# Two-tile feed-forwards opened tile by tile: h stationary, 512 weight columns moving, results turned

## The reference, cut to what matters

```python
def causal_depthwise_conv(u, w, b):        # 3 taps along the tokens, per column
    ...
def conv_glu_ffn(h, w_up_act, w_up_lin, w_conv, b_conv, w_down):
    a = causal_depthwise_conv(h @ w_up_act, w_conv, b_conv)
    return (jax.nn.gelu(a) * (h @ w_up_lin)) @ w_down
...
def _swiglu(h, wg, wu, wd):
    return (jax.nn.silu(h @ wg) * (h @ wu)) @ wd
```

## Time and profile before

| what | value |
|---|---|
| median of 3 runs | 2520.38 us (2516.61 to 2524.2) |
| the profiled execution | 2516.55 us, its span 2514.7 us |
| mean granted TensorE clock | 0.988 of full speed |
| TensorE matmul busy | 2418.3 us (96%) |
| VectorE busy | 1678.3 us (67%) |
| ScalarE busy | 1079.9 us (43%) |
| weight and modulation transfers | 418.55 MB, 49.7% of 16 DMA engines |

### The profile page before, as it was taken

One profiled execution on the slowest core, in us unless ns is written; L12 is line 12 of the kernel. 1 busy time (PEld: TensorE's weight loads), 2 busy tenths in 40 slices (PEclk: granted clock), 3 DMA queues, 4 the chain that ended last, 5 costly groups with the idle time before them and its releaser, 6 DMA issues.

```text
span 2514.7 us, 34853 instructions
## 1 busy us (share of the span) xinstructions
PE 2418.3 (96%) x13166; PEld 2033.5 (81%) x13166; DVE 1678.3 (67%) x2618; ACT 1079.9 (43%) x1850; POOL 390.8 (16%) x431
## 2 busy tenths in 40 slices
PE   6899999989999999999979999999999999999998
PEld 5678988779979888887648888889888888777997
DVE  6957987858995776777865565566565566356554
ACT  4566545566554212236744322224322225344543
POOL 1101101111111101105850110100100110001101
PEclk9999999999999999999989999999999999999999
DMA  8765895647783554543212463442353444322662
GB/s 322 248 174 188 306 322 201 220 117 247 262 278 115 184 191 173 191 153 93 68 34 84 135 197 120 164 171 94 128 203 125 155 170 114 120 90 77 194 201 93
DMA packets 135880, 422.57 MB, mean 168 GB/s; under 512 B 28448, under 2 KB 32672, under 8 KB 135712
## 3 DMA queue, kind: packets, MB, share of 16 engines
q1 hardware_dynamic: 135152, 418.55, 49.7%
q10 hardware_dynamic: 560, 1.79, 0.2%
HBM read 419.17 MB, written 1.11 MB: 167 GB/s over the span
## 4 chain that ended last, share of the span: by engine, by line
PE 66%; DVE 2%; ACT 1%; POOL 1%; issue 0%; POOLq 0%; DVEq 0%; ACTq 0%
PE ps L1141 20%; PE ps L1142 20%; PE ps L1143 20%; PE ps L1336 2%; PE ps L1324 1%; POOL ap L2208 1%; PE ps L1241 1%; PE ps L1293 1%; PE ps L1304 1%; DVE ps L2033 0%; PE ps L1359 0%; PE ps L1348 0%; ACT F L1458 0%; DVE sl L1687 0%; DVE hL L1776 0%
## 5 line engine op out<-in xcount | busy, mean ns | idle before, releaser
L1399 ACT ACTIVATE sh<-raw 128x1024 fp32r<-128x1024 f32 x534 | 551.6, 1043 | 907.1 <-PE ps L1143 880.2
L1141 PE MATMUL ps<-hH,sh 128*128 128x256 f32 (+1 forms) x2560 | 839.3, 328 | 3.7 <-DVE hL L1776 2.7
L1142 PE MATMUL ps<-hL,sh 128*128 128x256 f32 (+1 forms) x2560 | 834.5, 326 | 0.0
L1143 PE MATMUL ps<-hH,sl 128*128 128x256 f32 (+1 forms) x2560 | 834.5, 326 | 0.0
L1687 DVE TENSOR_TENSOR sl<-raw,sh 128x1024 fp32r<-128x1024 f32 x534 | 639.7, 1218 | 102.2 <-ACT sh L1399 101.9
L1141 PEld LDWEIGHTS ps<-hH,sh 128*128 128x128 f32 x2560 | 481.5, 188 | 55.5 <-issue 8.0
L1142 PEld LDWEIGHTS ps<-hL,sh 128*128 128x128 f32 x2560 | 480.7, 188 | 49.2 <-issue 1.7
L1143 PEld LDWEIGHTS ps<-hH,sl 128*128 128x128 f32 x2560 | 481.3, 188 | 48.2
L1701 DVE CUSTOM_DVE_ANT_0 mjunk<-raw,cB,V 128x1024 bf16<-128x1024 f32 x384 | 499.2, 1300 | 28.4 <-DMA C<-in_cst 8.4
L2181 POOL TENSOR_TENSOR uLl<-F,uHh 128x256 fp32r<-128x256 f32 (+1 forms) x132 | 168.1, 1274 | 1175.7 <-ACT uHh L1576 1068.0
L1141 PE MATMUL ps<-sh,uHh 128*128 128x512 f32 x792 | 311.8, 394 | 2.5 <-DVE sl L1687 2.5
(11 more groups left out here) (164 smaller groups left out, 2038.4 us busy)
## 6 DMA issues: line engine op xcount, KB each, us to landing
raw<-in_w SPq DMA_DIRECT2D x752, 512.0 KB, 4.7
G<-gates SPq DMA_DIRECT2D x14, 512.0 KB, 6.7
raw<-in_w SPq DMA_DIRECT2D x16, 256.0 KB, 4.5
cB<-in_rpb SPq DMA_DIRECT2D x64, 64.0 KB, 2.6
raw<-in_w SPq DMA_DIRECT2D x4, 492.0 KB, 5.9
S<-in_rows SPq DMA_DIRECT2D x6, 256.0 KB, 3.2
X<-in_x ACTq DMA_DIRECT2D x1, 1024.0 KB, 11.9
X<-in_ctx SPq DMA_DIRECT2D x1, 1024.0 KB, 6.0
```

What stands on the lines that cost most here:

```text
L1141: self.e.matmul(out, lh, rh, start=start, stop=False)
L1142: self.e.matmul(out, lh, rl, start=False, stop=False)
L1143: return self.e.matmul(out, ll, rh, start=False, stop=stop)
L1399: self.e.activation(self.m["sh"][k % SPL][:, 0:w], self.m["raw"][r % RAW][:, 0:w], ACT.Copy).then_inc(self.sems["w_hi"], 1)
```

## The change

In a two-tile feed-forward, column blocks 0 to 3 of both matrices are made in another way (`by_tile`). Their eight units are cut as two k-blocks by 512 columns. h of one tile is held stationary and 512 weight columns move, six matmuls for each unit and tile, so the result has tokens on its partitions. Each of the four results (two matrices, two tiles) is copied from PSUM to `S` (`utok`, two copies on ScalarE, two on VectorE) and turned back by four transposes (`uturn`) into four banks, each of which holds two column blocks. Tile 0 begins before tile 1 is turned: three units of `w_up_act` for tile 0, then tile 1's turn, then the fourth unit and two of `w_up_lin` for tile 0, and so on. In front of it stand 7 warming matmuls in `ffn1` and 14 in the last feed-forward, in place of 14 and 5.

The gated units of column blocks 0 to 3 follow beside column blocks 4 and 5 in `ffn1`: blocks 0, 1 and 4 beside block 4, and 2, 3 and 5 beside block 5. In the last feed-forward all four come one behind the other. `pace` is not called for the first four blocks; for the other 18 its argument is 2 x 22/18. The list `aside` begins with 5 empty entries instead of 8.

In the mixer's output projection, uppers are held back (`hold`) from the first use of tile 1 on; `ready` lets one go behind tile 0's split and one in front of tile 1's scaling, and `lowers` sends the owed lowers. Tile 0's split now stands ahead of tile 1's `gate2` (also in the down parts of `ffn1`, which share `gate_half`).

```diff
-    def norm_tile(self, hid, t, AB, s, st=None, wide=False, lag=0, early=False):
+    def norm_tile(self, hid, t, AB, s, st=None, wide=False, lag=0, early=False, held=False):
...
             self.second_parts()
+        if held:
+            self.add("lowers")
+            self.add("ready", n=1)
...
-    def gate_half(self, t, half, b, gid, AB, hid, st2):
+    def gate_half(self, t, half, b, gid, AB, hid, st2, held=False):
...
         self.rms_close(st2[t], 2)
+        self.second_parts()
+        if held and t:
+            self.add("ready", n=1)
...
-        self.norm_tile(hid, t, AB, 0, st, early=True)
+        self.norm_tile(hid, t, AB, 0, st, early=True, held=held and t)
...
                     part(kp, half, taken[(kp, half)], [i], i == 1, banks[half][i] if kp == 3 else None)
-                self.gate_half(i, half, banks[half][i], gid, AB, hid, st2)
+                    if i and not half and kp == 2:
+                        self.add("hold", on=True)
+                self.gate_half(i, half, banks[half][i], gid, AB, hid, st2, True)
...
+    def by_tile(self, names, hid, warm):
+
+        take = lambda n, j: self.unit(True, [n + (k, 0, 512) for k in (2 * j, 2 * j + 1)])
+
+        def part(n, j, t, b, last):
+            self.add("down", unit=n, ks=[2 * j, 2 * j + 1], tiles=[(t, (t, b))], last=last, full=b if j == 3 else None,
+                     act=("h", hid), nk=KD)
+
+        def stage(t, b, on):
+            S = self.place("S", 2 + t)
+            self.add("utok", b=b, S=S, on=on)
+            self.left(b)
+            return S
+
+        def turned(t, S, to):
+            self.add("uturn", S=S, t=t, to=to)
+
+        self.warm(warm)
+        self.add("hold", on=False)
+        one, two = ([take(n, j) for j in range(4)] for n in names)
+        A, B = [self.bank(), self.bank()], [self.bank(), self.bank()]
+        for j in range(3):
+            part(one[j], j, 0, A[0], False)
+        self.finish_norms()
+        part(one[3], 3, 0, A[0], False)
+        for j in range(2):
+            part(two[j], j, 0, B[0], False)
+        SA0 = stage(0, A[0], "a")
+        to = [self.bank(), self.bank()]
+        for j in range(4):
+            part(one[j], j, 1, A[1], True)
+            if j == 1:
+                turned(0, SA0, to)
+        for j in range(2):
+            part(two[j], j, 1, B[1], True)
+        SA1 = stage(1, A[1], "v")
+        for j in range(2, 4):
+            part(two[j], j, 0, B[0], False)
+        turned(1, SA1, to)
+        SB0 = stage(0, B[0], "a")
+        for j in range(2, 4):
+            part(two[j], j, 1, B[1], True)
+        up = [self.bank(), self.bank()]
+        turned(0, SB0, up)
+        SB1 = stage(1, B[1], "v")
+        return to, up, lambda: turned(1, SB1, up)
+
...
         self.rate = RATES[f"up{l}"]
-        self.warm(14)
-        self.finish_norms()
-        self.warm(5)
-        self.aside += [lambda: None] * 8
+        to, up, rest = self.by_tile((("w_up_act", l), ("w_up_lin", l)), hid, 7)
+        self.aside += [lambda: None] * 5
...
         def middle(g):
             g["f"] = self.next("F", 3)
             self.add("glu1_b", **g)
-            self.left(g["bu"])
-
-        for c in range(KF):
+            if g["c"] >= 4 or g["c"] % 2:
+                self.left(g["bu"])
+
+        def begin(c, ba, bu, o):
+            g = dict(l=l, c=c, ba=ba, bu=bu, o=o, s=self.place("S", c % 2), fid=fid, u=self.u_at)
+            self.add("glu1_a", **g)
+            if c >= 4 or c % 2:
+                self.left(ba)
+            late.extend([lambda g=g: middle(g), lambda g=g: self.add("glu1_c", **g)])
+
+        for c in range(4, KF):
             ba = self.product("w_up_act", l, c * 128, slice(0, 256), ("h", hid))
-            if late:
+            if c == 4:
+                rest()
+            if c in (4, 5):
+                while late:
+                    late.pop(0)()
+                begin(2 * c - 8, to[c - 4], up[c - 4], 0)
+            late.pop(0)()
+            bu = self.product("w_up_lin", l, c * 128, slice(0, 256), ("h", hid))
+            late.pop(0)()
+            if c in (4, 5):
+                begin(2 * c - 7, to[c - 4], up[c - 4], 256)
                 late.pop(0)()
-            bu = self.product("w_up_lin", l, c * 128, slice(0, 256), ("h", hid))
-            if late:
                 late.pop(0)()
-            g = dict(l=l, c=c, ba=ba, bu=bu, s=self.place("S", c % 2), fid=fid, u=self.u_at)
-            self.add("glu1_a", **g)
-            self.left(ba)
-            late = [lambda g=g: middle(g), lambda g=g: self.add("glu1_c", **g)]
-            self.pace(2)
+            begin(c, ba, bu, 0)
+            self.pace(2 * KF / (KF - 4))
...
         else:
-            self.warm(14)
-            self.finish_norms()
-            self.warm(5)
+            to, up, rest = self.by_tile((("ffn_w_gate_2", (l, half_i)), ("ffn_w_up_2", (l, half_i))), hid, 14)
...
+                if len(tiles) == 2 and cc < 4:
+                    ba, bu, o = to[c // 2], up[c // 2], 256 * (c % 2)
+                    if c == 0:
+                        rest()
+                    g = dict(N=N, c=c, ba=ba, bu=bu, o=o, s=self.place("S", c % 2), f=self.next("F", 3), fid=fid, u=self.u_at)
+                    if late:
+                        late.pop(0)()
+                    self.add("glu2_a", **g)
+                    if c % 2:
+                        self.left(ba, bu)
+                    late.append(lambda g=g: self.add("glu2_b", **g))
+                    continue
...
+        held, more = False, 0
         for s in self.steps:
             real = "unit" in s and s["kind"] != "place"
+            if s["kind"] == "hold":
+                held, more = s["on"], 0
+                continue
+            if s["kind"] == "ready":
+                more += s["n"]
+            if s["kind"] == "lowers":
+                out += lower
+                lower = []
+                continue
             if real:
                 out += lower
                 lower = []
-            if "unit" in s or "upto" in s:
+            if "unit" in s or "upto" in s or s["kind"] == "ready":
+                if s["kind"] == "ready":
+                    s["upto"] = len(self.units)
                 top = max(top, s["upto"] if "upto" in s else s["unit"] + 1)
                 while n < (len(self.units) if real else min(top, len(self.units))):
                     split, w, job = self.kinds[n]
                     if split and len(order) >= SPL and order[-SPL] not in used:
                         break
+                    if split and held and not (real and n <= s["unit"]):
+                        if not more:
+                            break
+                        more -= 1
                     if split:
                         out.append(dict(kind="upper", n=n, w=w))
                         lower.append(dict(kind="lower", n=n, w=w))
                         order.append(n)
                         loads.append(n)
                     n += 1
+            if s["kind"] == "ready":
+                continue
             if s["kind"] == "place":
                 job = self.kinds[s["unit"]][2]
...
+
+    def uturn(self, s):
+        t, S = s["t"], self.buf(s["S"])
+        if t == 0:
+            for b in s["to"]:
+                self.wait_ge(self.gone(b))
+        self.wait_ge(self.got("tok", s["S"]))
+        for c in range(4):
+            o = 256 * (c % 2) + 128 * t
+            x = self.e.transpose(self.buf(s["to"][c // 2])[:, o:o + 128], S[:, c * 128:(c + 1) * 128],
+                                 self.m["C"][:, C_ID:C_ID + 128])
+        x.then_inc(self.sems["tr"], 1)
+        self.done("tr", ("left", s["S"]), *([("full", b) for b in s["to"]] if t else []))
...
+    def utok(self, s):
+        if s["on"] != "a":
+            return
+        self.wait_ge(self.got("full", s["b"]))
+        self.wait_ge(self.gone(s["S"]))
+        self.e.copy(self.buf(s["S"])[:, :], self.buf(s["b"])[:, :]).then_inc(self.sems["a_ps"], 1)
+        self.done("a_ps", ("left", s["b"]), ("tok", s["S"]))
...
     def glu1_a(self, s):
-        l, c = s["l"], s["c"]
...
-        self.e.activation(self.buf(s["s"])[:, 0:256], self.buf(s["ba"])[:, 0:256], ACT.Identity,
+        self.e.activation(self.buf(s["s"])[:, 0:256], self.buf(s["ba"])[:, o:o + 256], ACT.Identity,
...
+    def utok(self, s):
+        if s["on"] != "v":
+            return
+        self.wait_ge(self.got("full", s["b"]))
+        self.wait_ge(self.gone(s["S"]))
+        self.e.tensor_copy(self.buf(s["S"])[:, :], self.buf(s["b"])[:, :]).then_inc(self.sems["v_ps"], 1)
+        self.done("v_ps", ("left", s["b"]), ("tok", s["S"]))
```

19 lines of the change are left out of this document (10 added, 9 removed).

## The result

The changed kernel takes 2557.41 us (median of 5 runs, 2555.86 to 2560.4) against 2520.38: ratio 1.0151, 95% interval 1.0133 to 1.0168, that is 37 us or 1.5% slower. The forecast was 2529.0 with a range up to 2537. The direction is right, the size is not: 8.6 us were forecast, and the profiled execution, with a span of 2555.6 against 2514.7, has 40.9.

The account below looks back on a forecast made before the run. VectorE's place in its list was taken to set layer 1's end. Layer 1 +11.4, layer 0 -1.5, last feed-forward -1.3 sum to +8.6 us: 2525.2 from the profiled 2516.55, 2529.0 as a median, range 2509 to 2537.

Parts of the forecast that it names:

- Held uppers cost nothing by themselves: Mixer's output projection: holding uppers back costs 0 us, as two units are prepared and TensorE warms beside it.
- Loads and bytes are the same: Whole kernel: the change moves the same loads and bytes, so no cost was counted for them.
- the 136.1 us list: Layer 1, VectorE's work from the next block to the down part's last lower: 146.8 us before, 136.1 after, ending at 759.5.
- Layer 1, forecast 11.4 us later: Layer 1's down part ends 11.4 us later, through late VectorE blocks and vector loads, though TensorE began 6.9 us sooner.
- the pile-up: Behind layer 1's opening, VectorE has 18.6 us of work plus about 7 us of chain waiting before the last `w_ada` block ends.
- Layer 0, forecast -1.5: Layer 0: opening gains 4.9 us on TensorE, 3.4 us lost behind the gate rows, so 1.5 us faster.
- Last feed-forward: Last feed-forward's opening: 32.4 us against 33.7, with 14 warmings kept in front, so 1.3 us faster.
- Sixteen transposes: Each opening: four groups of four at 0.5 us, 2.0 us in all; over 3 us would prove the opening's sum wrong.
- The gate row: Layer 0: VectorE's reserve is gone, so SP's wait for the rows through memory costs 3.4 us, bounds 0 and 6.
- Rival C: Vector-load stall stands before TensorE and halves its clock, 2 to 3 us each time: +16, 2536 us; chance 0.12.
- A: Openings keep their whole gain, VectorE's 11 us reserve absorbing pile-up and vector loads: -13.1, 2507.3 us; chance 0.18.
- B: Half the gain: layer 1 comes out even, layer 0 keeps 4.9: -6.2, 2514 us; chance 0.18.

Follow-up runs that it names:

- e11: The kernel before with the hold of uppers and its `ready` steps alone, `top` not raised, no turned opening: 2519.65 us, ratio 0.9994.
- e1: The changed kernel, but `ready` no longer raises the mark `top`: 2530.21 us, ratio 1.0042 to the kernel before.
- e6: e1 with the unawaited half of the conditioning vectors loaded at the start, the other ahead of the context tiles, silu in two halves: 2524.35 us, ratio 1.0024.
- e4: The changed kernel with `top` not raised (e1's edit) and modulation blocks paced beside the openings in `ffn1` too: 2514.89 us, ratio 0.998.
- e7: e4 with the feed-forward gate row's fetch three steps later (e5) and the conditioning vectors loaded earlier (e6): 2512.33 us, ratio 0.9978.
- e5: e4 with the fetch of the two layers' feed-forward gate row three steps later: 2511.63 us, ratio 0.9973.
- e12: e7 with the four turned columns' gated units beside columns 4 to 7, one each, instead of two each beside 4 and 5: 2512.46 us, ratio 0.9966.
- e10: e8 with the later gate row fetch (e5) and the earlier conditioning vectors (e6): 2512.83 us, ratio 0.9975.
- e8: The changed kernel with e1's edit and `ffn1` as before, so turned opening in the last feed-forward only, hold and `ready` kept: 2511.98 us, ratio 0.9977.
- e2: The kernel before with the mark `top` alone raised, from layer 0's out projection on: 2539.9 us, ratio 1.0084.
- e3: The changed kernel with modulation blocks paced beside the openings in `ffn1` too, `top` still raised: 2541.25 us, ratio 1.0089.

## Why the prediction was wrong, by its own steps

**"Held uppers cost nothing by themselves" and "Loads and bytes are the same": this is the step that failed.** The hold is free (e11, ratio 0.9994) and the bytes are the same; but I read `ready` as one upper let out, and did not follow the variable that it leaves behind. The order of VectorE's list was taken from the earlier trace rows, with one lower on each side of the product, and every sum behind it (5.1 us a column in layer 0, 5.7 in layer 1, the 136.1 us list) had that order in it. The diff held the cause in one line, and the price stood in the trace of before: of the steps between product and convolution, ScalarE's two and their hand-overs, only the lower of 1.14 us showed, because it covered them. It measured 0.94 us idle for each of 18 columns in each layer, and 27 us in all (e1 against the changed kernel), and by stage 25.6 of the 31.1 us between their profiled executions stand in the two up parts.

**Without that step the forecast is close.** It forecast 2529.0; e1 is the change as I had read it, and takes 2530.2 (by its ratio 10.6 us over the kernel before, forecast 8.6). That the sum comes so near is in part luck: the three stages below add up to 12.0, and 2.5 us come off between the conv module and the last T0, which the change doesn't touch. By stage, e1 against before in profiled executions:

- Layer 1, forecast 11.4 us later: 10.0 (T0 to conv, 613.0 against 603.0 us). The chain is the one forecast, a little shorter (its start is off by 0.9 us: it took the opening to end at T0 + 30.3, where the sum ahead of it has 30.8 and the trace 31.2): with T0 3.7 us later than before, the last `w_ada` block ends at 608.8 (forecast 608.9 + 3.7 = 612.6), the next one starts at 621.44 (623.4 + 3.7 = 627.1), and TensorE then stalls 9.31 us for a lower (forecast 5 to 10). VectorE is idle for 9.11 us in front of that block. The vectors' load is 3.6 to 4.5 us of the loss (e6); that the pile-up is the rest was not tried by itself. In the changed kernel itself this block starts at 639.96, past the 615 that would have spoken against the step; VectorE's idle time within the opening is 10.2 us (31.20 - 20.96), forecast 10.
- Layer 0, forecast -1.5: +3.5 (356.6 against 353.1). The opening gained 5.1 us on TensorE in e1 (30.7 against 35.8), 4.9 forecast, but 8.6 are lost behind it instead of 3.4. The term itself was well sized: TensorE waits 3.9 us for lowers there, 3.7 of it between 294.8 and 308.8, right behind the gate row's fetch at 291.74. What was put at nothing is the rest. Some 1.5 us are matmuls at the slower pace of 0.1178 us, which the profile of before doesn't have in this stage, 1.3 stand in the down part and the mixer of layer 1, where the kernels without the raised `top` have 219.3 to 222.1 us, and under 2 are not traced to anything. With blocks in the opening (e4) the layer costs 352.1, 1 us under before.
- Last feed-forward, forecast -1.3: -1.5. The 33.7 us of the sum should have been 33.9 (11.9 + 22.0), and so the forecast -1.5. Sixteen transposes: each group of four is 0.60 us in its row with the matmul behind it starting 0.36 later, so under 2.5 us an opening, well under the 3 us named as the test. Copies from PSUM: 0.69 us on VectorE (0.57 taken), beside matmuls.

**The gate row** cost as forecast, and more: in layer 0 VectorE stood 5.18 us for a load behind it and TensorE 5.13 (forecast 3.4, bounds 0 and 6). SP's queue in the changed kernel, with the send, three weight loads and the fetch, which waits for the send to land while nothing behind it can be issued:

```profile
282.79 0.48 SPq L1154 DMA_DIRECT2D gates<-gc  x1
286.00 1.94 SPq L1187 DMA_DIRECT2D raw<-in_w  x3
296.36 0.33 SPq L1168 DMA_DIRECT2D G<-gates  x1
```

With the columns mended (e4) there is enough reserve, and moving the fetch brings nothing that the times can tell.

**Rival C**, the half clock behind a stall, was real and came on top, in places that I had not named. After the 9.46 us stall in layer 1 the matmuls of the changed kernel start every 0.21 us instead of 0.115, and the granted clock from 644 to 652 is 0.62:

```profile
643.86 0.55 PE L1235 MATMUL ps<-hH,sh 128*128 128x256 f32 x1 [9.46 <-DVE sl L1802]
...
649.76 0.41 PE L1235 MATMUL ps<-hH,sh 128*128 128x256 f32 x1
649.97 0.32 PE L1236 MATMUL ps<-hL,sh 128*128 128x256 f32 x1
```

```profile
644.00:652.00 8.00, 8.00 (x46) 8.00 (x47) 6.99 (x11) 3.18 (x5) 0.73 (x1) 0.62 0.71 206
```

It lasts 6.1 us (643.86 to 649.97, granted clock 0.50, the lower of its two levels) for 29 matmuls, some 2.8 us dearer than at full clock. The Trainium skill (TensorE: Matmul & The Clock Gate, HAM oscillation) describes bursts of matmuls that start at half clock after idle gaps; the trace agrees for this stall. The forecast had said that it decides once a stall is as long as 3.74 us. In this kernel's up parts the clock is 0.50 behind the stalls of 9.46, 5.13 (304.3 to 308.7) and 3.49 us (692.3 to 697.8), and 1.00 behind the others, of at most 1.5 us: from 652 to 676, with two of 1.3 and 1.4 us in it, it is 1.00. In e1 it is 0.50 for 3.4 us behind a stall of 2.07 us as well. Whether TensorE's clock or VectorE's list ends later was not tried by itself: VectorE is nearly full from 644 on (6.99 of 8.0 us), so most of these 2.8 us may lie under its list.

**Rivals A and B**, the openings' gain kept in whole or half: with all mending e7, e5 and e12 stand at ratios of 0.9978, 0.9973 and 0.9966, 5 to 9 us under before, near B's 2514. But it is not the mechanism of A or B: e10 reaches the same without the two openings. What A overlooked in layer 1 stands in the second and third window of e5: an opening that takes TensorE's work away in front of a stage in which VectorE is the one that is full moves TensorE's idle time from before the stage into it.

**Not settled:** e8 and e10 are some 4 us under e11 by their ratios, and the stage of the last opening has 1.5 of it; the intervals allow that to be all. In layer 0's down part and layer 1's mixer e2, e3 and the changed kernel run 2.7, 5.7 and 5.8 us longer than before. Most of that is `top` again, for without it e4 has 5.8 us less there than e3, and e1 4.5 less than the changed kernel; by which wait it costs there is not traced.

## What to carry to other kernels

When a change touches a planner (the code that writes the order of all steps), follow the state that it leaves behind, not only the steps that it adds, and compare the order of each engine's list before and after: an instruction that fills the wait for another engine, moved to the other side of that wait, lays it bare in every turn of the loop (here 0.94 us in each of 36 columns, 27 us of the kernel's time). A mean load says little in an in-order queue; price the heaviest turn too (here the 7.18 us of a column with two blocks, in which five of TensorE's eight waits of layer 0 stand). And an opening shortened on one engine gains nothing if the stage behind it is bound by another, unless that other one is given work from its list during the opening: that was worth 15 us here, and the openings of layers 0 and 1 themselves nothing that the times can tell. And profiles of single executions settle a stage to some 4 us, no closer, unless the pace of the engine is compared first.

## What was not expected of the hardware

How exactly one instruction's place is paid: one lower before and one behind the product, or both before it, differ by 1.03 us a column, with the same work. Between the end of VectorE's product (261.61) and its convolution (262.55) ScalarE does the split of u (from 261.64) and the middle tap (0.55 us, to 262.52), so the 0.94 us are these two steps, with 0.03 us for each of the two hand-overs between the engines. And a send of 4 KB to memory takes 9.5 to 14.7 us to land in the changed kernel, where a weight load of 512 KB takes 4.9 (medians of 14 and 752: 12.9 and 4.9). SP's queue stands until its fetch may be issued, whatever is queued behind it: 6.3 to 10.8 us for the feed-forwards' gate rows of layers 0 and 1 in the kernel before, the changed one, e1 and e4.

And TensorE has two paces at full granted clock. These are the 18 columns of layer 0 in e8 and in e11, whose two kernels have the same steps there:

```profile
235.20:337.00 101.80, 101.80 (x867) 101.80 (x866) 88.49 (x132) 57.61 (x90) 14.85 (x18) 1.00 0.83 295
236.40:334.30 97.90, 97.90 (x866) 97.90 (x865) 87.97 (x132) 57.73 (x90) 16.85 (x18) 1.00 0.91 304
```

TensorE never stands in either, its clock is 1.00, and yet they are 3.9 us apart: the matmuls start every 0.1178 us in e8 and every 0.1133 in e11. In layer 1 it is the other way round, 97.9 us in e8 and 101.8 in e11, so it isn't the kernel. What sets it is open.
